# Stick-breaking mixer: the second group of query and key tiles is split into two groups, and taps and POOL's subtractions are re-ordered

## What is computed

```python
q = rms_norm(q.reshape(bsz, seq, 8, 64), q_norm_g)      # per token and head
k = rms_norm(k.reshape(bsz, seq, 8, 64), k_norm_g)
z = einsum("bqhd,bkhd->bhqk", q, k) * 64 ** -0.5
tail = reverse exclusive cumulative sum of where(s < t, log_sigmoid(-z), 0)
weights = where(s < t, exp(log_sigmoid(z) + tail), 0)
attn = einsum("bhqk,bkhd->bqhd", weights, v)

c = glu_a * sigmoid(glu_b)
c = causal_depthwise_conv(c, conv_dw_w, conv_dw_b)      # 31 taps
c = silu(layer_norm(c, conv_ln_g, conv_ln_b))
x = x + concatenate([attn, c]) @ w_out
```

## Time and profile before

| what | value |
|---|---|
| median of three runs | 1281.84 us (1280.19 to 1285.58) |
| the profiled execution | 1283.25 us, its span 1281.5 us |
| PE busy | 1232.8 us, 96% of the span |
| DVE, ACT, POOL busy | 591.4, 481.0, 532.4 us |
| mean granted clock | 0.979 |

### The profile page before, as it was taken

One profiled execution on the slowest core, in us unless ns is written; L12 is line 12 of the kernel. 1 busy time (PEld: TensorE's weight loads), 2 busy tenths in 40 slices (PEclk: granted clock), 3 DMA queues, 4 the chain that ended last, 5 costly groups with the idle time before them and its releaser, 6 DMA issues.

```text
span 1281.5 us, 15300 instructions
## 1 busy us (share of the span) xinstructions
PE 1232.8 (96%) x5681; PEld 997.2 (78%) x5681; DVE 591.4 (46%) x838; ACT 481.0 (38%) x698; POOL 532.4 (42%) x297
## 2 busy tenths in 40 slices
PE   7999979999999999999999988989999999999997
PEld 6876737788888888888877767777888888888886
DVE  5786964235545444100365566873354444541003
ACT  6233634434333333211455733434253333332112
POOL 3531211345444434444583224435353444444442
PEclk9998987999999999999999998999999999999999
DMA  5330110032333232322222212111233223322211
GB/s 178 124 99 33 33 33 33 33 100 98 98 98 98 92 105 77 108 92 93 90 92 81 66 33 66 34 34 48 84 99 98 98 98 98 115 98 99 99 66 66
DMA packets 84599, 105.39 MB, mean 82 GB/s; under 512 B 2020, under 2 KB 77131, under 8 KB 84555
## 3 DMA queue, kind: packets, MB, share of 16 engines
q1 hardware_dynamic: 84394, 104.53, 24.5%
q10 hardware_dynamic: 160, 0.26, 0.1%
HBM read 102.43 MB, written 2.10 MB: 82 GB/s over the span
## 4 chain that ended last, share of the span: by engine, by line
PE 81%; DVE 6%; issue 4%; ACT 4%; POOL 3%; DMA 1%; SPq 0%; POOLq 0%; ACTq 0%; DVEq 0%
PE ps L1487 16%; PE ps L1489 16%; PE ps L1488 16%; PE ps L1789 9%; PE ps L1784 9%; PE ps L1571 4%; PE ps L1965 3%; POOL w_lo L423 3%; PE ps L1918 2%; DVE cy L1053 2%; PE ps L1613 1%; ACT w_hi L550 1%; PE ps L1588 1%; DVE sp_lo L1088 1%; PE ps L1598 1%
## 5 line engine op out<-in xcount | busy, mean ns | idle before, releaser
L423 POOL TENSOR_TENSOR w_lo<-w_raw,w_hi 128x1024 fp32r<-128x1024 f32 x188 | 453.3, 2414 | 624.2 <-ACT w_hi L550 623.0
L1487 PE MATMUL ps<-h_hi,w_hi 128*128 128x512 f32 x936 | 371.2, 397 | 3.3 <-POOL w_lo L423 2.1
L1488 PE MATMUL ps<-h_lo,w_hi 128*128 128x512 f32 x936 | 365.3, 390 | 0.0
L1489 PE MATMUL ps<-h_hi,w_lo 128*128 128x512 f32 x936 | 365.3, 390 | 0.0
L550 ACT ACTIVATE w_hi<-w_raw 128x1024 fp32r<-128x1024 f32 x190 | 199.6, 1055 | 323.7 <-PE ps L1489 144.2
L1487 PEld LDWEIGHTS ps<-h_hi,w_hi 128*128 128x128 f32 x936 | 176.3, 188 | 45.2 <-issue 6.2
L1489 PEld LDWEIGHTS ps<-h_hi,w_lo 128*128 128x128 f32 x936 | 176.1, 188 | 37.1
L1488 PEld LDWEIGHTS ps<-h_lo,w_hi 128*128 128x128 f32 x936 | 176.2, 188 | 35.3 <-issue 0.5
L1179 DVE TENSOR_TENSOR ps<-ps,rbs 128x512 f32<-128x512 f32 x88 | 61.5, 699 | 172.0 <-PE ps L1489 171.6
L727 ACT ACTIVATE cv<-ps,par 128x512 f32<-128x512 f32 x44 | 34.3, 779 | 183.9 <-DVE ps L1179 161.9
L1145 DVE TENSOR_TENSOR xT<-xT,ps 128x512 f32<-128x512 f32 x24 | 16.4, 685 | 154.9 <-PE ps L1789 106.7
(11 more groups left out here) (276 smaller groups left out, 1715.3 us busy)
## 6 DMA issues: line engine op xcount, KB each, us to landing
w_raw<-in_w_up SPq DMA_DIRECT2D x33, 1024.0 KB, 5.1
w_raw<-in_w_down SPq DMA_DIRECT2D x22, 1024.0 KB, 4.8
w_raw<-in_w_in SPq DMA_DIRECT2D x21, 1024.0 KB, 5.2
w_raw<-in_w_gate SPq DMA_DIRECT2D x11, 1024.0 KB, 5.1
w_raw<-in_w_out SPq DMA_DIRECT2D x8, 1024.0 KB, 4.8
xtok<-in_x SPq DMA_DIRECT2D x4, 512.0 KB, 4.7
out_dram<-obuf SPq DMA_DIRECT2D x8, 256.0 KB, 2.1
sq<-in_final_norm_w SPq DMA_DIRECT2D x1, 512.0 KB, 6.1
```

The lines of the kernel that those rows point to most:

```text
L423: pool.tensor_tensor(unit_view(w_lo, at, down), unit_raw(at, down), unit_view(w_hi, at, down).bitcast(F32), ALU.subtract).then_inc(s_lo, 1)
L1487: pe.matmul(ps[:, bank, :], whi, hi, start=first, stop=False, skip_group_check=True)
L1488: pe.matmul(ps[:, bank, :], whi, lo, start=False, stop=False, skip_group_check=True)
L1489: mm = pe.matmul(ps[:, bank, :], wlo, hi, start=False, stop=last, skip_group_check=True)
```

## The change

The units 16 to 19 are multiplied in another order: query tile 2, key tile 6, query tile 3, key tile 7 (the places in `w_raw` stay, `raw_place` maps units 17 and 18 onto them). The second group becomes group 1 (tiles 2 and 6) and group 2 (tiles 3 and 7), each with its own `statistics`, root and scalings. On PE, the sums of group 1 stand ahead of the scores of heads 2 and 3, and its two spreads stand within and behind unit 19, in bank 7; those of group 2 stand behind `tails(2)` and behind the mean. On DVE, 40 instead of 20 tap instructions of half 1 stand ahead of `head(0)`, the taps end ahead of `head(2)`, `head(4)` stands between the last two scalings. On ACT, `scale_root(1)` stands ahead of `front(2)`, `take_qk(18)` ahead of `front(3)`. On POOL, the subtractions of units 18 and 19 wait for `s_spl` 2 (end of `head(1)`) and those of the first `w_out` units for `s_spl` 4 (end of `head(3)`). SP waits for `s_lo` 19 before the first load of `w_out`.

```diff
--- before.py
+++ after.py
@@ -39,8 +39,9 @@
 
 OUT_BANK = (0, 1, 2, 3, 6, 7, 2, 3)
 AH = 8
-GROUPS = ((0, 4, 1, 5), (2, 6, 3, 7))
-QK_TILE = {8: 0, 9: 1, 10: 4, 11: 5, 16: 2, 17: 3, 18: 6, 19: 7}
+SCALED = (0, 4, 1, 5, 2, 6, 3, 7)
+GROUP_UNITS = ((8, 9, 10, 11), (16, 17), (18, 19))
+QK_TILE = {8: 0, 9: 1, 10: 4, 11: 5, 16: 2, 17: 6, 18: 3, 19: 7}
 GC = 27
 
 
@@ -294,8 +295,13 @@
             b = 3 * (h % 2)
             return ps[:, b:b + 3, :].rearrange("p b n -> p (b n)")[:, 0:ZW]
 
+        def raw_place(u):
+
+            return {17: 18, 18: 17}.get(u, u)
+
         def unit_raw(u, down):
 
+            u = raw_place(u)
             pair = w_raw[:, (u // 2) % 2, :]
             if down:
                 return pair.rearrange("p (c n) -> p c n", c=2)[:, u % 2, :]
@@ -350,6 +356,7 @@
             sp.dma_start(sinkb[:], sinks_2.to_broadcast([P, 8])).then_inc(s_sink, 16)
             for n in range(2, len(in_cols)):
                 pair(n, cols(w_in, in_cols[n]))
+            sp.wait_ge(s_lo, 19)
             for n in range(4):
                 pair(U_OUT // 2 + n, cols(w_out, 256 * n))
 
@@ -446,7 +453,10 @@
             pool.wait_ge(s_const, 15)
             pool.affine_select(out=selT[:], in_=selT[:], compare_op=ALU.is_ge, fill=0.0, base=63,
                                pattern=[[-P, 8], [-1, P]], channel_multiplier=64).then_inc(s_const, 1)
-            rests(U_IN + 4, 16)
+            rests(U_IN + 4, 14)
+            pool.wait_ge(s_spl, 2)
+            rests(U_IN + 18, 2)
+            pool.wait_ge(s_spl, 4)
             rests(U_OUT, 4)
 
             inverse_root(1)
@@ -543,7 +553,7 @@
 
             def lead(at, i=0):
 
-                act.wait_ge(s_raw[(at // 2) % 2], 16 * (at // 4 + 1) + 16 * i)
+                act.wait_ge(s_raw[(raw_place(at) // 2) % 2], 16 * (at // 4 + 1) + 16 * i)
                 if at >= 4:
                     act.wait_ge(s_used, at + 4 * i - 3)
                 down = is_down(at)
@@ -654,26 +664,27 @@
             take_qk(17, 6)
             square_qk(17, 14)
             weights(1)
+            scale_root(1)
             front(2)
-            front(3)
             take_qk(18, 7)
             square_qk(18, 15)
+            front(3)
             take_qk(19, 6)
             square_qk(19, 16)
             weights(2)
             lead(20)
             lead(21)
-            scale_root(1)
+            scale_root(2)
             weights(3)
             attended_hi(0)
             front(4)
             front(5)
+            weights(4)
             attended_hi(1)
-            weights(4)
             weights(5)
             front(6)
             front(7)
-            act.wait_ge(s_qst, 2)
+            act.wait_ge(s_qst, 3)
             for c in range(CT):
                 act.wait_ge(s_lc, c + 1)
                 act.activation(sqk(c), cy[:, c, :], ACT.Square).then_inc(s_lsq, 1)
@@ -1061,7 +1072,7 @@
 
             def scale_variance(g):
                 dve.wait_ge(s_qst, g + 1)
-                link(dve.tensor_scalar(nvar[:, 0, :], ps[0:16, 4 + 2 * g, :], 1.0 / 64, EPS, ALU.mult, ALU.add), s_qv)
+                link(dve.tensor_scalar(nvar[:, 0, :], ps[0:16, 6 if g else 4, :], 1.0 / 64, EPS, ALU.mult, ALU.add), s_qv)
 
             def scale_refine(g):
                 dve.wait_ge(s_qr, 2 * g + 2)
@@ -1071,10 +1082,10 @@
                 link(dve.tensor_tensor(nvar[:, 1, :], nvar[:, 1, :], nvar[:, 2, :], ALU.mult), s_qv)
 
             def scale_qk(n):
-                g, j = n // 4, GROUPS[n // 4][n % 4]
+                j = SCALED[n]
                 w = gq8[:, 0:1] if j < 4 else par[:, 0, C_KG:C_KG + 1]
                 dve.wait_ge(s_qb, n + 1)
-                dve.scalar_tensor_tensor(qk[:, j, :], qk[:, j, :], w, ps[:, 4 + 2 * g + n % 2, :],
+                dve.scalar_tensor_tensor(qk[:, j, :], qk[:, j, :], w, ps[:, 4 + n % 2 if n < 4 else 7, :],
                                          ALU.mult, ALU.mult).then_inc(s_qn, 1)
 
             def head(h):
@@ -1103,28 +1114,29 @@
             dve.wait_ge(s_cdve, 5)
             for n in range(4):
                 scale_qk(n)
-            taps(1, 4, 14)
+            taps(1, 4, 24)
             head(0)
             head(1)
-            taps(1, 14, 23)
+            taps(1, 24, 29)
+            scale_variance(1)
+            taps(1, 29, 30)
+            scale_refine(1)
+            taps(1, 30, CK)
             head(2)
+            scale_qk(4)
             head(3)
-            taps(1, 23, 26)
-            scale_variance(1)
-            taps(1, 26, 27)
-            scale_refine(1)
-            scale_qk(4)
+            scale_qk(5)
+            scale_variance(2)
+            scale_refine(2)
             attended_lo(0)
-            scale_qk(5)
             scale_qk(6)
+            head(4)
             scale_qk(7)
-            taps(1, 27, CK)
-            head(4)
             head(5)
+            attended_lo(1)
             dve.wait_ge(s_mean, 1)
             for c in range(CT):
                 dve.tensor_tensor(cy[:, c, :], cy[:, c, :], ps[:, 6, :], ALU.subtract).then_inc(s_lc, 1)
-            attended_lo(1)
             head(6)
             head(7)
             attended_lo(2)
@@ -1575,17 +1587,22 @@
 
 
             def statistics(g, bank):
-                for n, u in enumerate(range(8 + 8 * g, 12 + 8 * g)):
-                    pe.wait_ge(s_qsq, 4 * g + n + 1)
-                    mm = pe.matmul(ps[0:16, bank, :], sel[:, QK_TILE[u], :], sqk(n), start=(n == 0), stop=(n == 3))
+                us = GROUP_UNITS[g]
+                for n, u in enumerate(us):
+                    pe.wait_ge(s_qsq, (0, 4, 6)[g] + n + 1)
+                    mm = pe.matmul(ps[0:16, bank, :], sel[:, QK_TILE[u], :], sqk(u % 4), start=(n == 0),
+                                   stop=(n == len(us) - 1))
                 mm.then_inc(s_qst, 1)
 
             def spread_scale(n):
-                g, j = n // 4, GROUPS[n // 4][n % 4]
+                g = 0 if n < 4 else n // 2 - 1
                 pe.wait_ge(s_qv, 5 * g + 5)
-                if n % 4 >= 2:
+                if n in (2, 3):
                     pe.wait_ge(s_qn, n - 1)
-                pe.matmul(ps[:, 4 + 2 * g + n % 2, :], selT[:, j, :], nvar[:, 1, :], start=True, stop=True).then_inc(s_qb, 1)
+                if n in (5, 7):
+                    pe.wait_ge(s_qn, n)
+                pe.matmul(ps[:, 4 + n % 2 if n < 4 else 7, :], selT[:, SCALED[n], :], nvar[:, 1, :],
+                          start=True, stop=True).then_inc(s_qb, 1)
 
             def scores(heads):
 
@@ -1667,29 +1684,34 @@
             tails(1)
             pe.wait_ge(s_take, 13)
             part(18, 7, range(2))
+            pe.wait_ge(s_take, 14)
+            statistics(1, 6)
             scores((2, 3))
             part(18, 7, range(2, 8))
-            pe.wait_ge(s_take, 14)
-            part(19, 6, range(8))
+            pe.wait_ge(s_qv, 6)
+            part(19, 6, range(3))
+            pe.wait_ge(s_take, 15)
+            spread_scale(4)
+            part(19, 6, range(3, 8))
+            spread_scale(5)
             tails(2)
             pe.wait_ge(s_take, 16)
-            statistics(1, 6)
+            statistics(2, 6)
             tails(3)
+            pe.wait_ge(s_qn, 6)
             outputs(0)
-            spread_scale(4)
-            pe.wait_ge(s_mlo, 1)
-            spread_scale(5)
-            pe.wait_ge(s_qn, 6)
             scores((4, 5))
-            spread_scale(6)
-            spread_scale(7)
-            pe.wait_ge(s_qn, 8)
-            outputs(1)
+            pe.wait_ge(s_qv, 11)
             pe.wait_ge(s_tap, 4 * CK)
             for c in range(CT):
                 mm = pe.matmul(ps[:, 6, :], lnone[:], cy[:, c, :], start=(c == 0), stop=(c == CT - 1))
             mm.then_inc(s_mean, 1)
+            pe.wait_ge(s_mlo, 1)
+            spread_scale(6)
+            spread_scale(7)
             tails(4)
+            pe.wait_ge(s_qn, 8)
+            outputs(1)
             tails(5)
             scores((6,))
             scores((7,))

```

## The result

| | median | runs | ratio to before (95%) |
|---|---|---|---|
| before | 1282.56 us (1280.19 to 1285.58) | 4 | |
| after | 1289.1 us (1288.48 to 1290.37) | 4 | 1.0053 (1.0033 to 1.0072) |

The change made the kernel slower by 6.5 us by the medians. That lies above the range, and beyond the 0.5% on its slow side. The profiled execution took 1288.48 us with a span of 1286.8, so 5.3 us of span more.

The account below looks back on a forecast made before the run. PE waits for DVE; head 6's scores set the end. PE, 12 us late by tails(3), regains 10 at the roots; a tails(4) wait replaces the mean's: 2 us slower, 1285.2 us (1283.8 from the median), range 1278.5 to 1288.5.

Parts of the forecast that it names:

- What bounds the kernel: Between 164.8 and 186.0 PE waits for DVE; the start of head 6's scores, 196.91 before, carries the difference to the end.
- the twenty taps: Ahead of head(0): 13.3 us of taps plus 4.2 of stretch beside POOL, head(0) at 135.5, PE waits 9.9 us.
- rival (a): Taps ahead of head(0) don't stretch: it starts at 131.3, PE waits 5.8 us, 1280 us in all; chance 0.12.
- signs of being wrong: PE's wait ahead of tails(0) under 5 us, PE still waiting at the roots, or the clock at 0.50 beyond 145.
- the planned 139.4: Start of tails(0) on PE, held from 129.44 until head(0) ends on DVE: a new wait of 9.9 us.
- the planned 198.7: Start of head 6's scores, when tails(5) ends, against 196.91 before: 1.8, say 2 us later.
- units 18 and 19 beside ten taps: Their POOL subtractions after head(1) stretch ten tap instructions by 4.2 us, to 10.9; unit 18's subtraction stays hidden.
- no wait at the spreads of group 1: Around unit 19 on PE: roots are there at 158.8, the first spread needs them at 161.8, 3 us to spare.
- the mean without a wait: Behind scores(4,5) on PE: taps end at 160, so the mean follows at once, a wait of 2.93 us less.
- PE's new wait ahead of tails(4): PE waits 2.8 us for head(4), which stands behind scale_qk(6) on DVE until 189.1.
- SP's wait and the second root hidden: First w_out load delayed to about 146, needed about 170; second refine stretched to 177.7, due by 183.5; neither delays PE.
- rival (c): The clock stays low long after the 9.9 us wait, through tails(0) and beyond: 1287.5 to 1291 us; chance 0.10.

Follow-up runs that it names:

- the kernel with gaps: The kernel after, with a one-column DVE memset that reads nothing behind each pair of the taps 14 to 23; 1287.56 us, ratio 1.0040.

## Why the prediction was wrong

**What bounds the kernel** was right: PE waits for DVE there, and the date of head 6's scores carries the difference. It moved from 196.84 to 203.24, 6.4 us, and the span grew by 5.3. The difference of 1.1 arises right behind, by the clock: the tails of head 6 run slow from their start in before and in the kernel after only from 215.3.

**The step that failed** is the one on the twenty taps. It took the meeting of a tap and a subtraction for a stretch of 2.1 us on DVE, once for each subtraction, and had no term for a wait of PE ahead of unit 16. In place of this POOL was shut out: unit 16 came at 133.45, where 2.8 us from its start would have been about 121.5, and PE waited 11.89 us for it, while head(0) began at 131.16 and not at 135.5. The prediction's own rival (a), taps that don't stretch, was seen as a gain of 3.7 us; it is the sign of the worse case. The same rows bore both readings: a tap of 2868 ns shows that POOL was let in once, not that it always is. That PE has 8.3 us of work between unit 16 and tails(0) was in the plan, but only as work beside the wait. With POOL shut out it all comes behind: tails(0) at 143.41, 4.0 us behind the planned 139.4. One of the prediction's signs of being wrong came up here: no wait of PE stands ahead of tails(0), which was to be 9.9 us.

**Sizes.** Head 6's scores came 4.5 us behind the planned 198.7. Of these, 0.7 was there before the stretch (scores of heads 0 and 1 at 118.46 for 117.75). Of the 4.0 at tails(0), which hold that 0.7, 2.2 besides it are left at tails(2) (170.09 for 167.2), since the slower clock, for which I had put 1.5 us behind tails(0), was over by about 137, ahead of it; 0.3 more at tails(4) (192.45 for 189.2). The last 1.3 came behind tails(4), where PE took 10.8 us to the scores (192.45 to 203.24) for 9.5 planned, with its clock low. The medians lie 6.5 us apart and the two profiled executions 5.2; the remaining 1.3 is that the profiled execution of before lies 0.7 above its median and that of the kernel after 0.6 below.

**Right:** units 18 and 19 beside ten taps (10.99 us for 10.9); no wait at the spreads of group 1; the mean without a wait; PE's new wait ahead of tails(4), 2.60 us for 2.8; SP's wait and the second root hidden, the refine stretched once, by 2 us (an operation of 2.73 us), for nothing. So the gain that the plan had behind tails(0) arrived nearly in full: from there to head 6's scores it is 59.8 us, where 59.3 were planned and before takes 67.4. The time measured, 1289.1, lies in the band of rival (c), the low clock, but not by its mechanism: in the kernel after the clock was back at 1.00 about 3.4 us behind the wait, ahead of tails(0). Where the wait did come ahead of tails(0), in the kernel with gaps, the clock outlasted the first tails, and (c) is what happened in the profiled execution.

## What to carry to other kernels

Two engines that keep each other out of SBUF need not take turns. Before a long unbroken run of vector operations with two operands in SBUF is moved, ask what POOL must deliver while it lasts, and who waits for that. Then either issue that work from the vector engine, or break the run; a memset that reads nothing was enough here. The first brought 4 to 6 us; the second, by the medians, 1.5 us, which these intervals don't tell from nothing. And work that had stood beside a wait counts only if the wait doesn't move ahead of it.

## What the runs showed of the hardware

The taps meant here are those with two operands in SBUF, 0.75 us each. POOL's subtraction (2.37 us alone) took 14.1, 16.4, 12.7, 18.0, 14.0 and 8.7 us when it was asked for in the seventh or a later tap of a long run, and 2.8 to 2.9 us when it was asked for in the first, fourth or fifth tap of a run or where one memset of 0.06 us stood between taps. The Trainium skill (SBUF — State Buffer, section "SBUF: two separate sides") says that the one who starts first has the port pair for the whole instruction and the other blocks. For one instruction the traces agree (a tap of 2899 ns). They show besides that a row of instructions can keep the other engine out for as long as it lasts: 15.7 us at the most here, 18.02 less the 2.36 that the subtraction takes.

The clock makes executions of one kernel differ ahead of the change too. Windows from 104 to 121.2 of the kernel before, and of the one with the short memset on POOL:

```profile
104.00:121.20 17.20, 16.28 (x71) 12.72 (x71) 14.00 (x21) 3.59 (x5) 2.53 (x2) 0.88 0.00 1
```

```profile
104.00:121.20 17.20, 13.05 (x66) 10.16 (x64) 17.20 (x27) 6.75 (x7) 5.77 (x2) 1.00 0.00 0
```

With the clock at 0.88 the scores of heads 0 and 1 begin at 117.75, with 1.00 at 114.53. Nothing ahead of them differs on PE's list. A difference of 3 us between single executions is no finding, and most of the intervals above are wider than that.
